# The last FFN of a hybrid decoder step: a gate unit moved ahead of the down products, and down tiles added from PSUM by VectorE

## What is computed

```python
def half_ffn(x, g, w_gate, w_up, w_down):
    h = rmsnorm(x, g)
    return x + 0.5 * ((jax.nn.silu(h @ w_gate) * (h @ w_up)) @ w_down)
y = rmsnorm(half_ffn(x, g_ffn2, ...), g_final)
```

## Time and profile before

| | |
|---|---|
| runs | 3 |
| median | 3013.39 us |
| lowest and highest | 3008.59 and 3025.14 us |
| profiled execution: span from its first to its last instruction | 3018.0 us |
| TensorE busy in it | 2743.8 us (91%) |
| VectorE, ScalarE, GpSimd busy in it | 1732.8, 908.3, 598.7 us |

### The profile page before, as it was taken

One profiled execution on the slowest core, in us unless ns is written; L12 is line 12 of the kernel. 1 busy time (PEld: TensorE's weight loads), 2 busy tenths in 40 slices (PEclk: granted clock), 3 DMA queues, 4 the chain that ended last, 5 costly groups with the idle time before them and its releaser, 6 DMA issues. The chain is left out here.

```text
span 3018.0 us, 44859 instructions
## 1 busy us (share of the span) xinstructions
PE 2743.8 (91%) x15387; PEld 2215.2 (73%) x15387; DVE 1732.8 (57%) x2290; ACT 908.3 (30%) x1701; POOL 598.7 (20%) x845
## 2 busy tenths in 40 slices
PE   6778899999999999988869789978999999999997
PEld 4456666666666677865526789954989999999997
DVE  7549999898898937777452554382252222222226
ACT  4221211221111114049613633131053333332334
POOL 1010032222222301200211000050013322222223
PEclk8779999999999999999878899999999999999999
DMA  9866699989898825511296531053011111111111
GB/s 359 302 219 195 194 323 315 315 309 312 313 301 293 302 87 177 166 56 29 102 276 207 175 98 36 22 196 126 29 50 43 42 43 54 42 42 48 42 42 57
DMA packets 334117, 478.20 MB, mean 158 GB/s; under 512 B 26600, under 2 KB 215397, under 8 KB 332110
## 3 DMA queue, kind: packets, MB, share of 16 engines
q1 hardware_dynamic: 291110, 333.29, 33.3%
q0 software_dynamic: 42416, 142.32, 13.9%
q10 hardware_dynamic: 408, 0.31, 0.0%
HBM read 453.22 MB, written 22.62 MB: 158 GB/s over the span
## 5 line engine op out<-in xcount | busy, mean ns | idle before, releaser
L88 DVE TENSOR_TENSOR wlo<-raw,whi 128x1024 fp32r<-128x1024 f32 (+1 forms) x184 | 220.9, 1210 | 409.4 <-ACT whi L84 409.3
L1957 POOL TENSOR_TENSOR xT<-xT,ffn_down 128x344 f32<-128x344 f32 x264 | 249.2, 946 | 714.3 <-ACT ffn_down L2001 710.0
L111 PE MATMUL banks<-ffn_ghi,whi 128*128 128x344 f32 (+1 forms) x880 | 323.4, 367 | 66.1 <-DVE ffn_glo L1749 31.0
L84 ACT ACTIVATE whi<-raw 128x1024 fp32r<-128x1024 f32 (+1 forms) x184 | 189.1, 1040 | 544.9 <-PE banks L113 413.3
L111 PE MATMUL banks<-ffn_hhi,whi 128*128 128x344 f32 x1056 | 339.3, 321 | 8.2 <-DVE ffn_hlo L141 5.4
L609 POOL DMA_DIRECT2D ffn_vt<-in_cache_v_dram x384 | 206.0, 537 | 683.5 <-issue 681.0
L112 PE MATMUL banks<-ffn_hlo,whi 128*128 128x344 f32 x1056 | 338.0, 320 | 0.0
L113 PE MATMUL banks<-ffn_hhi,wlo 128*128 128x344 f32 x1056 | 337.9, 320 | 0.0
L113 PE MATMUL banks<-ffn_ghi,wlo 128*128 128x344 f32 (+1 forms) x880 | 316.0, 359 | 0.0
L112 PE MATMUL banks<-ffn_glo,whi 128*128 128x344 f32 (+1 forms) x880 | 315.3, 358 | 0.0
L111 PE MATMUL banks<-a_hhi,whi 128*128 128x512 f32 x704 | 288.3, 410 | 12.8 <-DVE wlo L88 12.8
(11 more groups left out here) (475 smaller groups left out, 4911.5 us busy)
## 6 DMA issues: line engine op xcount, KB each, us to landing
ffn_kt<-in_cache_k_dram SPq DMA_DIRECT2D x448, 256.0 KB, 4.4
ffn_vt<-in_cache_v_dram POOLq DMA_DIRECT2D x384, 256.0 KB, 4.9
raw<-in_w_ffn_gate_dram SPq DMA_DIRECT2D x44, 512.0 KB, 4.0
raw<-in_w_ffn_up_dram SPq DMA_DIRECT2D x44, 512.0 KB, 4.1
raw<-in_w_ffn_down_dram SPq DMA_DIRECT2D x44, 512.0 KB, 4.7
last_kt<-in_cache_k_dram POOLq DMA_DIRECT2D x64, 256.0 KB, 3.1
s_vt<-in_cache_v_dram POOLq DMA_DIRECT2D x64, 256.0 KB, 5.4
s_vt<-in_cache_v_dram SPq DMA_DIRECT2D x64, 256.0 KB, 5.2
```

The lines of the kernel that those rows point to most:

```text
L84: act.activation(self.k.whi[c % W_RING][:, 0:self.width], self.slots[s][:, 0:self.width], ACT.Copy).then_inc(self.hi_done, 1)
L88: dve.tensor_tensor(self.k.wlo[c % W_RING][:, 0:self.width], self.slots[self.slot(n, c)][:, 0:self.width], self.k.whi[c % W_RING][:, 0:sel ...
L111: pe.matmul(out, whi, rhi, start=first, stop=False)
L1957: pool.tensor_tensor(x, x, dt_[:, m % DR, 0:n], ALU.add).then_inc(added, 1)
```

## The change

It is confined to `ffn` and `Final`.

- TensorE does the next group's first gate unit ahead of this group's down tiles. Gate 0 of group 0 stands before the loop; a group is then up 0, gate 1, up 1, gate 0 of the next group, down tiles. The last group has no next gate unit. The loads on SP, the hi and lo conversions, the takeouts (`gates`) and silus are put in the same order, and the slots of the down weights change with it.
- The down tiles go by turns to five banks: 6, 7 and the three up banks (`DOWN = 4 * (OWN + UP) + 2 * OWN`). Down tile m waits for the add of the last tile in its bank; the first tiles in up banks wait for the takeout of the last up unit; the next group's up 0 waits for the last add in its bank.
- VectorE adds a down tile straight from PSUM to `xT` with one scalar_tensor_tensor (x + 0.5 * bank). ScalarE's copy and GpSimd's add are gone, and GpSimd has no work in this stage.
- The conversion of the next up weight's lo part stands behind the fourth add; the next group's second gate weight is converted behind the last down tile.
- In the last group the final gain moves from VectorE to ScalarE, behind the square of the same tile, and VectorE sums the squares of tile m - 1 behind the add of tile m.

```diff
-    def columns(self, v, x_added, before):
-        for m in range(len(self.tiles) * KD):
-            t, k = divmod(m, KD)
-            t0, n = self.tiles[t]
-            j = m - t - 1
-            v.wait_ge(x_added, before + m + 1)
-            v.tensor_scalar(self.scaled[:, k, t0:t0 + n], self.k.xT[:, k, t0:t0 + n], self.k.gains[:, 5, k:k + 1], None,
-                            ALU.mult).then_inc(self.gained, 1)
-            if k:
-                v.wait_ge(self.squared, m + 1)
-                if k > 1:
-                    v.wait_ge(self.added, j)
-                v.tensor_tensor(self.acc[:, t, 0:n], self.acc[:, t, 0:n], self.square[:, j % 2, 0:n], ALU.add).then_inc(self.added, 1)
+    def gain_of(self, act, m):
+        t, k = divmod(m, KD)
+        t0, n = self.tiles[t]
+        act.activation(self.scaled[:, k, t0:t0 + n], self.k.xT[:, k, t0:t0 + n], ACT.Copy,
+                       scale=self.k.gains[:, 5, k:k + 1]).then_inc(self.gained, 1)
+
+    def add_of(self, v, m):
+        t, k = divmod(m, KD)
+        n = self.tiles[t][1]
+        j = m - t - 1
+        if k:
+            v.wait_ge(self.squared, m + 1)
+            if k > 1:
+                v.wait_ge(self.added, j)
+            v.tensor_tensor(self.acc[:, t, 0:n], self.acc[:, t, 0:n], self.square[:, j % 2, 0:n], ALU.add).then_inc(self.added, 1)
...
-        dt_ = self.at(f"{name}_down", [P, T, tiles[0][1]])
-        DR = 2
         GATE = list(range(T))
         UP = list(range(T, 2 * T))
-        DOWN = [2 * T, 2 * T + 1]
+        OWN = [2 * T, 2 * T + 1]
+
+        DOWN = 4 * (OWN + UP) + 2 * OWN
+        same_bank = lambda m: [x for x in range(m) if DOWN[x] == DOWN[m]]
+        last_down = lambda bank: max(m for m in range(TILES_DOWN) if DOWN[m] == bank)
...
                 def body(i, last):
+                    def load(c, src, parts):
+                        w.load(sp, i * 6 + c, c, src, parts)
+                    load(1, gate_unit(up, i, 0), 8)
+                    load(2, gate_unit(gate, i, 1), 8)
+                    load(3, gate_unit(up, i, 1), 8)
+                    if not last:
+                        load(4, gate_unit(gate, i + 1, 0), 8)
+                        load(5, down_unit(i, 0), 1)
+                        load(6, down_unit(i, 1), 1)
+                    else:
+                        load(4, down_unit(i, 0), 1)
+                        load(5, down_unit(i, 1), 1)
+                w.load(sp, 0, 0, gate_unit(gate, 0, 0), 8)
...
-            @block.gpsimd
-            def _(pool):
-                pool.sem_inc(added, DR)
-
-                def body(i, last):
-                    for m in range(TILES_DOWN):
-                        t, k = divmod(m, KD)
-                        t0, n = tiles[t]
-                        x = self.xT[:, k, t0:t0 + n]
-                        pool.wait_ge(drained, i * TILES_DOWN + (m + 3))
-                        pool.tensor_tensor(x, x, dt_[:, m % DR, 0:n], ALU.add).then_inc(added, 1)
-                groups(pool, body)
...
-                        w.hi(act, i * 6 + 2, 2, i * 3 + 2, down_ps, i * TILES_DOWN + 1)
-                    silus(i, 0)
-                    w.hi(act, i * 6 + 3, 3, i * 3 + 2, gate_ps, i * (2 * T) + T)
+                        hi(i, 2, down_ps, i * TILES_DOWN + 1)
+                        hi(i, 3, down_ps, i * TILES_DOWN + 1)
+                    else:
+                        hi(i, 3, gate_ps, T)
                     g_his(i, 0)
-                    w.hi(act, i * 6 + 4, 4, i * 3 + 3, up_ps, i * (2 * T) + T)
+                    hi(i, 4, up_ps, i * (2 * T) + T)
                     silus(i, 1)
-                    w.hi(act, i * 6 + 5, 5, i * 3 + 3, gate_ps, i * (2 * T) + 2 * T)
+                    hi(i, 5, gate_ps, i * (2 * T) + 2 * T)
                     g_his(i, 1)
                     if not last:
-                        w.hi(act, i * 6 + 6, 0, i * 3 + 4, up_ps, i * (2 * T) + 2 * T)
-                    for m in range(TILES_DOWN):
-                        n = tiles[m // KD][1]
-                        act.wait_ge(down_ps, i * TILES_DOWN + (m + 2))
-                        act.wait_ge(added, i * TILES_DOWN + (m + 1))
-                        act.activation(dt_[:, m % DR, 0:n], ps[DOWN[m % 2]][:, 0:n], ACT.Copy,
-                                       scale=0.5).then_inc(drained, 1)
-                        if last and m >= 2:
-                            act.wait_ge(added, i * TILES_DOWN + (m - 2 + 1 + DR))
-                            final.square_of(act, m - 2)
-                    if not last:
-                        w.hi(act, i * 6 + 7, 1, i * 3 + 4, down_ps, i * TILES_DOWN + (TILES_DOWN + 1))
+                        hi(i, 6, up_ps, i * (2 * T) + 2 * T)
+                        silus(i + 1, 0)
+                        hi(i, 7, gate_ps, i * (2 * T) + 3 * T)
+                    else:
+                        for m in range(TILES_DOWN):
+                            act.wait_ge(added, i * TILES_DOWN + (m + 1))
+                            final.square_of(act, m)
+                            final.gain_of(act, m)
+                silus(0, 0)
                 groups(act, body)
-                for m in (TILES_DOWN - 2, TILES_DOWN - 1):
-                    act.wait_ge(added, (GROUPS - 1) * TILES_DOWN + m + 1 + DR)
-                    final.square_of(act, m)
                 final.act(act)
...
+                def drain(i, m):
+                    t, k = divmod(m, KD)
+                    t0, n = tiles[t]
+                    x = self.xT[:, k, t0:t0 + n]
+                    v.wait_ge(down_ps, i * TILES_DOWN + (m + 2))
+                    v.scalar_tensor_tensor(out=x, in0=ps[DOWN[m]][:, 0:n], scalar=0.5, in1=x, op0=ALU.mult,
+                                           op1=ALU.add).then_inc(added, 1)
+
                 def body(i, last):
                     if not isinstance(i, int) or i:
                         w.lo(v, i * 6 + 2, 2)
-                    gates(i, 0)
                     w.lo(v, i * 6 + 3, 3)
                     gs(i, 0)
                     w.lo(v, i * 6 + 4, 4)
...
                     gs(i, 1)
                     if not last:
                         w.lo(v, i * 6 + 6, 0)
-                        w.lo(v, i * 6 + 7, 1)
+                        gates(i + 1, 0)
+                    for m in range(TILES_DOWN):
+                        drain(i, m)
+                        if m == 3 and not last:
+                            w.lo(v, i * 6 + 7, 1)
+                        if last and m:
+                            final.add_of(v, m - 1)
+                gates(0, 0)
                 groups(v, body)
-                final.columns(v, added, (GROUPS - 1) * TILES_DOWN + DR)
+                final.add_of(v, TILES_DOWN - 1)
                 final.dve(v)
...
-                def unit(i, c):
-
-                    f, is_up = divmod(c, 2)
-                    w.ready(pe, i * 6 + c)
-                    for t, (t0, n) in enumerate(tiles):
+                def unit(i, n, c, f, is_up):
+
+                    first = isinstance(i, int) and i == 0 and f == 0
+                    w.ready(pe, n)
+                    for t, (t0, size) in enumerate(tiles):
 
                         pe.wait_ge(up_r if is_up else gate_r, i * (2 * T) + (f * T + t + 1))
                         bank = (UP if is_up else GATE)[t]
+                        if is_up and f == 0 and not first:
+                            pe.wait_ge(added, i * TILES_DOWN - (TILES_DOWN - 1 - last_down(bank)))
                         for k in range(KD):
-                            if isinstance(i, int) and i == 0 and c == 0:
+                            if first and not is_up:
                                 late.operand(pe, t, k)
-                            last = three_passes(pe, ps[bank][:, 0:n], self.whi[c % 3][:, k * P:(k + 1) * P],
-                                                self.wlo[c % 3][:, k * P:(k + 1) * P], hhi[:, k, t0:t0 + n],
-                                                hlo[:, k, t0:t0 + n], k == 0, k == KD - 1)
+                            last = three_passes(pe, ps[bank][:, 0:size], self.whi[c % 3][:, k * P:(k + 1) * P],
+                                                self.wlo[c % 3][:, k * P:(k + 1) * P], hhi[:, k, t0:t0 + size],
+                                                hlo[:, k, t0:t0 + size], k == 0, k == KD - 1)
                         last.then_inc(up_ps if is_up else gate_ps, 1)
-                        if isinstance(i, int) and i == 0 and c == 1:
+                        if first and is_up:
                             late.sums(pe, t)
+
                 def body(i, last):
-                    for c in range(4):
-                        unit(i, c)
-                    w.ready(pe, i * 6 + 4)
-                    w.ready(pe, i * 6 + 5)
+                    unit(i, i * 6 + 1, 1, 0, True)
+                    unit(i, i * 6 + 2, 2, 1, False)
+                    unit(i, i * 6 + 3, 3, 1, True)
+                    if not last:
```

(26 more changed lines are left out.)

13 lines of the change are left out of this document (removed).

## The result

| | before | after |
|---|---|---|
| median | 3010.99 us (4 runs, 2995.3 to 3025.1) | 2966.5 us (4 runs, 2960.4 to 2970.6) |
| ratio of after to before | | 0.985, 95% interval 0.982 to 0.988 |
| span of the profiled execution | 3018.0 us | 2958.7 us |

The kernel is faster by 44.5 us, or 1.5%; 45.2 us and 2968 us were forecast. A second batch gave 2964.2 us (6 runs) against 3012.9 us, a ratio of 0.985 (0.982 to 0.988).

What follows compares the result with a forecast made beforehand. TensorE was taken to bound the last FFN. Gap 25.0, clock 10.2 and last group with end 10.0 sum to 45.2 us, off the median of 3013.4: 2968 us, range 2960 to 2987.

Steps and rivals of the forecast that it cites:

- Part 1: Ten of eleven last-FFN groups: a gate unit before the down products removes TensorE's 2.5 us wait, 25.0 us.
- Nothing late next: Last-FFN groups: moved weight conversions, loads and the up unit's new wait for adds stay covered, costed at nothing.
- rival (c): TensorE waits 2.5 us per group elsewhere, at first up or second gate unit; slow stretches stay; 3003 us; chance 0.05.
- Part 2: Behind the removed gaps of ten groups: seven slow-clock stretches of 1.46 us go, 10.2 us, bounds 0 to 10.2.
- Rival (a): Down products through five banks: the clock falls anyway, 1.46 us in each of ten groups, 2983 us; chance 0.07.
- Part 3: Down tiles of the first ten groups: VectorE's adds from PSUM, 0.51 us each, cost nothing.
- rival (b): Down stretch: late adds hold up TensorE; 3021 us at 1.24 us each, gain all given back at 1.21; chance 0.03.
- Part 4: Last group and end: down stretch 6.1 us less, final roots 3.9 us sooner, 10.0 us, bounds 7.4 to 11.5.

Runs made afterwards that it cites:

- e6 to e8: Changed kernel with one wait each, putting gaps of 1.3, 2.3 and 3.5 us before the first ten groups' down products: 2980.0, 2995.8 and 2996.0 us.
- the adds-only kernel: Kernel before, in its old order, with VectorE's adds from five banks and the final gain on ScalarE: 2999.7 us, ratio 0.997.

## Why the prediction was right, point by point

**Part 1, the gap: right, a little small.** 25.0 us were forecast; e6 to e8 and the windows give 10 x (70.72 - 67.96) = 27.6. The term was mis-sized: I counted the wait as listed, 2.50 us. It is listed from the end of the last matmul, but a matmul that follows without a gap starts 0.16 us before that end (its time in the row is 0.32, the distance between starts 0.16), and the first one behind a gap takes 0.10 longer (0.42 for 0.32). 2.50 + 0.16 + 0.10 = 2.76.

**Nothing late next: right.** No wait of TensorE appears in the ten groups. The rival (c), that the wait moves, is refuted by the waits view.

**Part 2, the clock: right.** 7 x 1.46 = 10.2 us were forecast; all of the ten groups have 1.00, and 71.73 - 70.72 = 1.01 per group is 10.1 us. That the slow stretches follow the gaps, which I had argued from the earlier trace rows, is shown by the kernels that put gaps back: with no gap there is none in ten groups, and with gaps of 2.3 us there are eight. How many follow is not a matter of the gap's length alone, and seven of ten behind 2.5 us was a count from one execution, which I carried over and did not explain. Rival (a), slow stretches without a gap because of five banks, is refuted: the adds-only kernel walks through five banks and has them only behind its gaps, and the changed kernel has none in ten groups. The rule of the Trainium skill (TensorE: Matmul & The Clock Gate, A second HAM failure mode: psum-queue depth-cycling), by which a kernel that cycles through banks and idles briefly in between has its clock oscillate, does not show here. The adds-only kernel does idle between its groups of matmuls, and with five banks it has seven slow stretches in ten groups, as the kernel before has with two.

**Part 3, the adds free of charge: right for the changed kernel, but my margin was wrong.** The adds take 0.517 us and TensorE never waits for one. The price of the rival (b) was too low: its slack of four tiles is lost at product 22, where the list of banks ends 6, 7, 6, 7. With 0.4 in the place of 3.8 and 21 adds in the place of 24, adds of 1.24 us would have cost 11 x 7.3 = 80 us and not 53, and the break-even is near 1.09 us, not 1.21. Both are estimates by the formula, without the slow stretches that such waits can bring. The kernel with three adds, 1.52 us, is slower than before, as this rival says.

**Part 4, the end: right.** 10.0 us were forecast and 11.0 measured. The down stretch went from 30.48 to 24.50 us, 6.0 of 6.1 forecast. Roots begin 1.45 us behind the last product, as forecast; the tail from there takes 18.0 us instead of 19.1, the 1.1 us more. That tail varied by 1.6 us between two executions of the same kernel, so I don't look for a cause. VectorE and ScalarE kept pace: the last add, square and gain start 0.93 to 0.94 us behind those before them, and VectorE's acc add starts 0.44 us behind an add of 0.52 (2938.30 and 2938.74 in the timeline). The Trainium skill (VectorE: DVE Perf Modes, The DRAIN you can't avoid) says that the next operation does not start until the pipe is empty; the trace does not agree with that. The same section adds that a next operation that is not held starts earlier, which the prediction left out and which these starts fit.

**The sum.** 45.2 us against 44.5 by the medians, and 50.0 by the stage in two single executions, of which 1.3 us lie at its start and can't be told from scatter. The forecast was right because each term was: 27.6 for 25.0, 10.1 for 10.2, 11.0 for 10.0. These make 48.7, as do the medians of the second batch (3012.9 less 2964.2), so that 45.2 meets 44.5 to within 1 us is luck of the scatter in the first. What I had not seen is that Parts 1 and 3 need each other: the order alone would have brought 12 us less, because the conversion and the silu it moves stand in front of ScalarE's copies.

## What to carry to other kernels

A gap that repeats in each group costs what the waits view lists, and a bit more (0.26 us here), and may also cost a stretch at the lower clock level; both go when any work of TensorE's covers it, a whole unit or 15 matmuls whose operands are ready. When work is moved on one engine's queue, look at what its helpers must now do at the new place, and who waits behind that in their queues: here two edits are worth 48.7 us together, and 25.6 and 11.1, 36.7 in sum, each by itself. When banks are given out by a list, the slack is that of the closest repeat in it, its end included, not of the usual distance.

## What the runs showed that I had not expected

- How often a gap is followed by a slow stretch depends on more than its length: 0 of 10 behind 1.3 us, 8 of 10 behind 2.3 us, 7 of 10 behind 2.5 us, but 2 of 10 behind 3.5 us with groups of 71.70 us, and 10 of 10 behind the same 3.5 us with 0.47 us more work in each group. Each count is from one execution of a kernel, that for 2.5 us from one each of two kernels.
- With no gap, groups repeat to 0.01 us (67.96), while the stages ahead of this one, in unchanged code, differ by up to 18 us between executions (this stage starts between 2167 and 2185 us, and at 2186 before the change). A stage is the better yardstick for an edit of this size.
- Instructions of VectorE and ScalarE overlap with the next of their own queue: 0.43 to 0.44 us from start to start for 0.51 to 0.52 us on VectorE, and on ScalarE 0.40 for a square of 0.49 and 0.47 for a gain of 0.57.
